# Nine weight blocks (three experts ahead) in one shared tensor, three slices of a modulation set computed in the routing gap, and expert borders with fewer register loads, in a two-layer inference step

## What is computed

```
for layer in (0, 1):
    shift, scale, gate = split(silu(c) @ w_ada[layer, 0] + b_ada[layer, 0], 3)   # c per sequence, w_ada is 1024 x 3072
    h = x * (1 + scale) + shift
    m = mixer(h)            # layer 0: gated linear attention beside a convolution; layer 1: pooling mixer
    x = layer_norm(ALPHA * x + (1 + gate) * m)
    shift, scale, gate = split(silu(c) @ w_ada[layer, 1] + b_ada[layer, 1], 3)
    h = x * (1 + scale) + shift
    comb = top-1 group of 4, then top-2 of its 4 experts, as weights      # 264 x 16
    m = sum over e of 16: ((silu(h @ w_gate[e]) * (h @ w_up[e])) * comb[:, e]) @ w_down[e]
    x = layer_norm(ALPHA * x + (1 + gate) * m)
```

## Time and profile before

| | us |
|---|---|
| median of 3 runs (lowest to highest) | 929.91 (926.99 to 933.59) |
| the profiled execution | 925.51 |
| its span in the profile | 923.7 |
| experts of layer 0 (24 chunks): first `gate_up` to the last `down`'s end | 246.30 to 509.41 |
| experts of layer 1 (25 chunks): the same | 637.42 to 891.46 |
| PE busy, share of the span | 86% |
| q1, the queue of SP's transfers | 271.74 MB, 74.7% of the span |

### The profile page before, as it was taken

One profiled execution on the slowest core, in us unless ns is written; L12 is line 12 of the kernel. 1 busy time (PEld: TensorE's weight loads), 2 busy tenths in 40 slices (PEclk: granted clock), 3 DMA queues, 4 the chain that ended last, 5 costly groups with the idle time before them and its releaser, 6 DMA issues.

```text
span 923.7 us, 22581 instructions
## 1 busy us (share of the span) xinstructions
PE 794.0 (86%) x9194; PEld 477.0 (52%) x9195; DVE 422.7 (46%) x1133; ACT 280.2 (30%) x562; POOL 129.6 (14%) x215
## 2 busy tenths in 40 slices
PE   4799999998699998797978879976999769999984
PEld 2478885784354444343433558743544434444443
DVE  1159988426344443333333461263444314444453
ACT  2045583314132322222221250141323112323323
POOL 0251777000011000000000000001010000101001
PEclk9799997999699999899988989997999979999997
DMA  9996633459307889999999999393699999998601
GB/s 321 381 261 234 223 141 106 172 191 390 149 0 285 345 360 421 420 425 419 427 416 411 360 388 370 144 382 137 274 377 418 428 418 426 420 420 364 272 0 47
DMA packets 63880, 280.39 MB, mean 304 GB/s; under 512 B 3013, under 2 KB 3627, under 8 KB 55638
## 3 DMA queue, kind: packets, MB, share of 16 engines
q1 hardware_dynamic: 60738, 271.74, 74.7%
q0 software_dynamic: 2432, 6.94, 2.5%
q10 hardware_dynamic: 676, 1.24, 0.4%
HBM read 277.47 MB, written 3.37 MB: 304 GB/s over the span
## 4 chain that ended last, share of the span: by engine, by line
PE 68%; DMA 20%; DVE 4%; issue 3%; ACT 3%; SPq 1%; POOL 0%; POOLq 0%; DVEq 0%; ACTq 0%
PE bank L605 18%; DMA ring<-in_w_up 15%; PE bank L715 8%; PE bank L615 7%; PE bank L854 6%; PE bank L577 6%; PE bank L627 6%; DMA ring<-in_w_ada 5%; PE bank L471 3%; PE bank L585 2%; PE bank L520 1%; PE bank L490 1%; PE bank L549 1%; PE bank L733 1%; DVE t L1191 1%
## 5 line engine op out<-in xcount | busy, mean ns | idle before, releaser
L605 PE MATMUL bank<-ring,work 128*32 128x256 f32 x3136 | 207.0, 408 | 60.7 <-DMA ring<-in_w_up 42.0
L605 PEld LDWEIGHTS bank<-ring,work 128*32 128x32 f32 x3136 | 106.0, 116 | 149.7 <-issue 105.4
L1609 DVE SCALAR_TENSOR_TENSOR x<-bank,ada,x 128x256 f32<-128x256 f32 x392 | 162.0, 476 | 0.0
L1606 DVE TENSOR_TENSOR work<-work,bank 128x32 f32<-128x32 f32 x98 | 18.4, 188 | 278.0 <-PE bank L627 278.0
L1765 POOL TENSOR_TENSOR work<-t 128x192 f32<-128x192 f32 x51 | 26.5, 519 | 618.4 <-PE bank L577 456.6
L615 PE MATMUL bank<-ring,work 128*32 128x256 f32 x1568 | 94.8, 382 | 0.0
L577 PE MATMUL bank<-htm,work 128*32 128x256 f32 (+1 forms) x1224 | 84.8, 391 | 9.6 <-POOL work L1768 9.6
L627 PE MATMUL bank<-work 32*128 32x264 f32 x816 | 77.6, 451 | 4.9 <-DVE x L1191 3.9
L1127 ACT ACTIVATE work<-bank 128x128 f32<-128x128 f32 x49 | 13.6, 278 | 217.4 <-PE bank L605 217.4
L715 PE MATMUL bank<-h,ring 128*128 128x264 f32 x320 | 73.9, 389 | 0.0
L715 PEld LDWEIGHTS bank<-h,ring 128*128 128x128 f32 x320 | 60.0, 190 | 11.5 <-issue 0.8
(11 more groups left out here) (242 smaller groups left out, 882.8 us busy)
## 6 DMA issues: line engine op xcount, KB each, us to landing
ring<-in_w_gate SPq DMA_DIRECT2D x32, 2048.0 KB, 13.0
ring<-in_w_up SPq DMA_DIRECT2D x32, 2048.0 KB, 16.4
ring<-in_w_down SPq DMA_DIRECT2D x32, 2048.0 KB, 17.5
ring<-in_w_ada SPq DMA_DIRECT2D x24, 2048.0 KB, 19.9
ring<-in_w_in_even SPq DMA_DIRECT2D x5, 2048.0 KB, 33.0
ring<-in_w_out_even SPq DMA_DIRECT2D x2, 2048.0 KB, 9.2
ring<-in_w_out_odd SPq DMA_DIRECT2D x2, 2048.0 KB, 20.8
htm<-in_x_prompt ACTq DMA_DIRECT2D x1, 1024.0 KB
```

Source lines behind the costliest of these rows:

```text
L605: last = mm(GU[C * q:C * (q + 1), :].rearrange("p (a n) -> p a n", a=2), hgc[:, P * (k % 2) + C * (k // 2):P * (k % 2) + C * (k // 2 + 1)] ...
L1609: last = v.scalar_tensor_tensor(out=x[:, i, 0:SEQ], in0=bank[4 + dq][:, 0:SEQ], scalar=gate[:, i, 0:1], in1=x[:, i, 0:SEQ], op0=ALU.mult, ...
```

## The change

- `big` is one SBUF tensor that holds `work`, `acc`, `t2` and `h`. Three further slots, 6 to 8, lie over its columns 3200 to 15488 (`late`): slots 6 and 7 over `work` and `acc`, slot 8 over `t2` and `h`. They are only used for experts. `prow` moves to `htm`, and POOL's fill of `htm` with zeros behind the first mixer's stores goes away.
- The order of the units and their slots is written out (`load_plan`, `PLAN`). Experts go through three sets of three slots (`SETS`), so expert e is issued once expert e-3 is done. Gate and up of an expert count on one semaphore.
- Before the experts of layer 0 SP issues, behind ada 11: ada 12, the gate of expert 1, ada 13, the up of expert 1, ada 14, gate and up of expert 0, the downs of experts 1 and 0, and expert 2. In layer 1 it is experts 0, 1 and 2, too.
- Units 12 to 14 are computed around `ranks(0)`; DVE takes them in with `ada_copy(2, 0)` behind the routing. Unit 15 alone is left behind the experts, and behind `layer_norm_var(1)`. PE waits for the copy before its first `turn`, since both use bank 3.
- Unit 7 is computed ahead of the output projection, unit 8 where unit 7 was, unit 10 ahead of the logits.
- In the first mixer the sums over the 256 prompt columns of the attention's output, and unit 4, come ahead of the products with the sample states; a table warm-up of ACT comes one step earlier; the final state has bank 0.
- In the expert loop on PE one number of the table is loaded per expert in place of two, and the counts to wait for are worked out once in three experts. Expert 15 stands behind the loop.

The diff, cut to its core:

```diff
@@ units, slots and the plan
-U_PRE = 19
+NSLOT = 9
 RING = 6
+LATE0 = 3200
+SETS = [[(4, 5, 0), (6, 7, 8), (1, 2, 3)], [(6, 7, 8), (0, 1, 2), (3, 4, 5)]]
+PIECES = [(0, 0, 4), (0, 4, 6), (1, 0, 4), (1, 4, 6), (2, 0, 3), (2, 3, 4), (2, 4, 6), (3, 0, 4), (3, 4, 6)]
+def load_plan():
+    plan = [(("ada", i), i) for i in range(4)]
...
+    plan += [(("ada", 12), 1), ((0, 1, 0), 6), (("ada", 13), 2), ((0, 1, 1), 7), (("ada", 14), 3), ((0, 0, 0), 4),
+             ((0, 0, 1), 5), ((0, 1, 2), 8), ((0, 0, 2), 0)]
+    plan += [((0, e, i), SETS[0][e % 3][i]) for e in range(2, EXPERTS) for i in range(3)]
+    plan += [(("ada", 15), 1), (("ada", 16), 2), (("ada", 17), 3), (("out1", 0), 4), (("out1", 1), 5), (("ada", 18), 0),
...
@@ SBUF
-        h = sb("h", [P, KD, T])
-        t2 = sb("t2", [P, KD, T])
-        acc = sb("acc", [P, KD, T])
-        work = sb("work", [P, 9152])
+        big = sb("big", [P, 9152 + 128 + 3 * KD * T])
+        work = big[:, 0:9152]
+        acc, t2, h = (big[:, a:a + KD * T].rearrange("p (k t) -> p k t", k=KD)
+                      for a in (9152, 9152 + KD * T + 128, 9152 + 2 * KD * T + 128))
+        late = big[:, LATE0:LATE0 + 3 * 4096].rearrange("p (s n) -> p s n", s=3)
@@ SP
             def fill_rest(l):
                 sp.wait_ge(M[l]["table_ready"], l + 1)
-                with sp.Fori(1, EXPERTS // 2) as ep:
-                    for j in range(2):
-                        e = sp.snap(2 * ep + j)
-                        chunks = sp.value_load(tab[l][0:1, bass.ds(e - 1, 1)], min_val=1, max_val=MAXCH)
+                with sp.Fori(1, EXPERTS // 3) as ep:
+                    for j in range(3):
+                        e = sp.snap(3 * ep + j)
+                        chunks = sp.value_load(tab[l][0:1, bass.ds(e - 2, 1)], min_val=1, max_val=MAXCH)
...
+            sp.wait_ge(E("mix0_stored"), 1)
+            sp.wait_ge(E("out0_src"), KD)
+            fill_expert(0, 1, 0)
+            unit_free(sp, ("ada", 13))
+            fill(("ada", 13))
+            sp.wait_ge(E("out0_done"), KD)
+            fill_expert(0, 1, 1)
+            unit_free(sp, ("ada", 14))
+            fill(("ada", 14))
+            for i in range(2):
+                unit_free(sp, (0, 0, i))
+                fill_expert(0, 0, i)
+            sp.wait_ge(E("tm_tr"), 2 * TT)
+            fill_expert(0, 1, 2)
+            unit_free(sp, (0, 0, 2))
+            fill_expert(0, 0, 2)
+            for i in range(3):
+                unit_free(sp, (0, 2, i))
+                fill_expert(0, 2, i)
@@ PE, expert loop
+                if l == 0:
+                    pe.wait_ge(E("ada_copied"), 5)
                 turn(1)
...
-                        lo = pe.value_load(tab[l][0:1, bass.ds(2 * ep + j, 1)], min_val=0, max_val=MAXCH)
-                        hi = pe.value_load(tab[l][0:1, bass.ds(2 * ep + j + 1, 1)], min_val=1, max_val=MAXCH)
-                        filled = [pe.snap((ep + ((u + i) // RING + 1)) * 16) for i in range(3)]
+                with pe.Fori(0, EXPERTS // 3) as ep:
+                    both_filled, filled = ([pe.snap(n * (ep + SET_FILLS[l][j])) for j in range(2)] for n in (32, 16))
+                    lo = bound(bass.ds(3 * ep, 1))
+                    for j in range(3):
+                        hi = bound(bass.ds(3 * ep + j + 1, 1))
+                        expert(j, lo, hi, both_filled[min(j, 1)], filled[min(j, 1)])
+                        lo = hi
@@ PE, around the routing of layer 0 and behind its experts
-            projection("out0", 0, U_OE, acc, 0, "out0_src", {})
             ada_unit(7)
+            projection("out0", 0, acc, 0, "out0_src", {})
+            ada_unit(8)
             layer_norm_var(0)
-            ada_unit(8)
             ada_unit(9)
             ada_columns()
+            ada_unit(10)
...
-            ada_unit(10)
             ada_unit(11)
+            pe.wait_ge(E("tm_a"), 4)
+            ada_unit(12)
+            ranks(0)
+            ada_unit(13)
+            ada_unit(14)
             ada_columns()
-            ranks(0)
             moe(0)
-            ada_unit(12)
             layer_norm_sum_x(1)
-            ada_unit(13)
             layer_norm_var(1)
-            ada_unit(14)
             ada_unit(15)
             ada_columns()
@@ DVE
             routing(0)
+            ada_copy(2, 0)
             moe(0)
```

281 lines of the change are left out of this document (149 added, 132 removed).

## The result

| | before | after |
|---|---|---|
| median (lowest to highest), us | 931.50 (926.99 to 933.59), 4 runs | 895.56 (893.59 to 897.72), 4 runs |
| ratio of the times | 1 | 0.9646, 95% interval 0.9605 to 0.9688 |
| the profiled execution | 925.51 | 897.72 |
| its span | 923.7 | 895.9 |

The changed kernel is 3.5% faster, 2.6 us from the forecast of 893. In a second set of runs it had 894.2 us beside 927.84 (13 runs of before), ratio 0.9642 (0.9587 to 0.9697).

The account below looks back on a forecast made before the run. The transfer queue was taken to bound the long middle of both expert stages, with PE following. Terms +1.1 - 15.0 - 5.4 - 15.0 - 1.8 = -36.1 us gave a forecast of 893 us, range 878 to 906.

Parts of the forecast that it names:

- Three experts ahead: Expert stages: expert 2 moves into the queue's idle window, one expert less in the queue-bound part; -15.0 us in each layer.
- Behind the experts: Layer 0, last `down` to first `h`: unit 15 starts earlier, 22.5 us in place of 27.9, so -5.4 us.
- The way to the first expert: Stretch up to layer 0's first `gate_up`: preloads and later projection cost +1.1 us in all, ends -2 and +10.
- Does it all fit ahead of the first chunk?: Preloads before layer 0's experts: start slips 0.3 us and first down 0.8, so +1.1 us.
- the next part: Front and routing gap: unit 7 +1.7, one unit fewer -2.5, units 13 and 14 +0.3; counted as 0, ends -3 and +3.
- PE's own gain on the way there: Before layer 0's experts: only unit 9 left behind the sum of squares, one unit goes, -2.5 us.
- The projection's slip: First mixer's output projection: unit 7 ahead of it, less some 0.7 us from earlier norm sums and warm-up, +1.7 us.
- Borders: Between experts on PE: one of two table loads goes; counts only behind layer 1's last wait, -1.8 us, ends 0 and -8.
- (a): Rival: preloads ahead of layer 0's experts collide, expert 0's down lands 10 us later; 903 us, chance 0.09.
- (b): Rival: the queue also loses its gaps in the expert stages, 8 us more in layer 0, 5 in layer 1; 880, chance 0.07.
- (c): Rival: late slots come free too late in layer 1, so its 15 us are lost; 908 us, chance 0.06.
- (d): Rival: PE must fetch code for the larger expert loop, at 3.5 us a border 18 us slower; 948 us, chance 0.04.

Follow-up runs that it names:

- x2: The changed kernel, but expert 2 is issued in the loop once expert 0 is done, so only two experts ahead: 924.9 us, ratio 0.9961.
- x4: The changed kernel with only half of the down matrix of layer 0's experts 3 to 15 transferred, the rest stale: 861.6 us in one run.
- x8: The changed kernel with six filling products, which nobody reads, around the last two scatters of each layer: 891.83 us, ratio 0.9613.
- x5: The changed kernel with SP's queue reordered: units 12 to 14, then expert 0 whole, then experts 1 and 2: 890.09 us, ratio 0.9592.
- x6: The changed kernel with unit 5 moved into PE's wait ahead of the column sums, units 6 and 7 one place forward: 890.89 us, ratio 0.9605.
- x9: The changed kernel with the edits of x5, x6 and x8 together: 881.36 us, ratio 0.9497.

## Why the prediction was right, and where it was not

**Three experts ahead: right.** -15.0 in layer 0 against -15.1, and in layer 1 -15.0 and -1.8 against -16.4. The reason given is the reason: x2 gives back the gain of the stages and leaves the rest, x4 shows that PE can do layer 0 in 222 us under the 247, and the last wait of layer 1 came 14.6 us earlier. The queue's idle time was forecast as 270 to 280; it was some 10 us, from 275.6 (expert 2's down, issued at 248.59, landed 27.0 us later) to expert 3's issue at 286.03.

**Behind the experts: right, with a wrong price inside.** The 27.9 us of the prediction's profile go from the last `down`'s start to `h`; in after it is 21.9 + 1.9 = 23.8, forecast 22.5. The missing 1.3 us is the clock: I took the norm's length from layer 1, where the sums L512 took 5.39 us, and in after they took 6.84. In neither place does a unit stand ahead of them, and without one they scatter between 5.25 and 6.84 us; with unit 12 among them before had 4.21 in layer 0. x8 shows that 3.8 is to be had. That the difference between the means is 5.4 all the same is because before waits longer there on average than in its first profile.

**The way to the first expert: the step that failed.** +1.1 was forecast and +6.6 came, by the means. Between the two profiles the first `gate_up` came at 252.3, where 246.6 was forecast: 5.7 us too late. Two things were wrong.

The larger is the output projection's slip, put at +1.7 and measured at 4.9 between the two profiles. It passes on in full: ada 11 is issued 31.0 us after the projection starts in before (200.46 and 169.46) and in after (205.32 and 174.34), and all seven blocks stand behind it. That is 3.2 of the 5.7 us.

The other is a consumer that was left out. "Does it all fit ahead of the first chunk?" compared only expert 0's blocks with the first `gate_up`, and the next part gave units 13 and 14 +0.3, as work inside a wait. It never asked when unit 14's weights land. By the prediction's own numbers that is 208.6 + 3 x 5.4 + 2 x 5.0 + 1.7 = 236.5. PE gets to unit 14 62.4 us after the projection starts (238.36 in after, where it ends with a slow unit 13, is 64.0; the second profile of after, x4 and x5 have 62.4), so with the projection where the prediction had it at 169.5 + 1.7 + 62.4 = 233.6. A wait of 2.9 us was due, and from the end of the wait to the first `gate_up` it is 11.3 us in after: 236.5 + 11.3 = 247.8 in place of 246.6, another 1.2 us. The rest, some 1.2 us, is that the blocks up to unit 14 took a little longer than reckoned. Its landing, from the issues at 221 and 230 (unit 14, and the up matrix of expert 0):

```profile
ring<-in_w_ada SPq DMA_DIRECT2D x1, 2048.0 KB, 19.7
...
ring<-in_w_up SPq DMA_DIRECT2D x1, 2048.0 KB, 20.4
```

Issued at 221.08, unit 14 landed 19.7 us later, at 240.8, and the gather behind it ran at 245.50. Expert 0's up matrix landed at 230.22 + 20.4 = 250.6 (forecast 246.6), 1.7 us before PE used it. So unit 14 was the last that the first chunk waited for, and the up matrix was close behind. x5 brings both forward and the whole 6.6 us are gone (244.4 against 245.3), though its projection is still 4.3 us later than the mean of before (168.6). PE's own gain on the way there, forecast as -2.5, is real, and larger: from the projection to the first `gate_up` it is 71.5 us in x5 and 76.8 in before. The two ends for this term were -2 and +10, and the +6.6 is inside.

**The projection's slip: mis-sized.** +1.7 was forecast, 4.9 came between the two profiles and 5.5 between the means. 3.3 of it is unit 7, which stands ahead of the projection now: it was reckoned as 2.4, but it waits 0.48 us for ACT and takes 2.37 us for 1.94. 0.9 is unit 6 (2.86 us for 1.93). The 0.7 that was to come back did come, as column sums that start 1.2 us earlier than in the first profile of before, but they take 1.8 us longer, so that 0.6 is lost in place of it. x6 wins back 3.6 by taking one unit out of this chain and putting it into the wait for DVE ahead of it.

**Borders: right inside the loop, too cheap at its end.** 0.2 and 0.7 us were forecast; measured are 0.05 inside the loop and 326.86 - 323.91 - 1.75 = 1.20 at its end. Each is some 0.1 to 0.75 us less than before's 0.8 and 1.3, so the loop's end was put 0.5 too low. Only the borders behind layer 1's last wait count, and they are 1.8 us shorter, the -1.8 of the sum; where the chunk behind that wait starts cold, 1.6 of it goes again.

**The rivals.** (a) is half true: the first chunk did slip, by 6.6 and not 10, yet by the late projection and unit 14's weights, and little by slower blocks or expert 0's down. The seven blocks took 37.3 us (213.3 to 250.6) where 36.3 were forecast. (b) is false, the slow slices are still there. (c) is false, layer 1 gained all of its 15 us. (d) is false: the border inside the loop is 1.80 us with three bodies, and the loop's end 2.95 for 3.02.

**By the medians.** 929.9 - 36.1 was within 2 us of 895.56, and that is partly luck: the term ahead of the experts was 5.5 us too good, and the profile behind the sum was 1.7 us of span under the mean of three, with the shortest norm and second mixer of them. The means of the spans differ by 31.4, the medians by 33.6 and 35.9 in the two sets. Where the remaining 2.2 to 4.5 us of the medians lie, no profile shows.

## What to carry to other kernels

Where a queue bounds a stage, look for the time in which it stands still before the stage, and count in blocks of queue: one expert moved into that window was worth one expert's transfer here, 15 us in each layer. Check every consumer of what is moved, not only the first and the last: a small step (unit 14) whose block stands behind others in an in-order queue can hold up the chain as well as the blocks of the stage itself. And where the queue's start hangs on a step of PE (the projection here), a unit put ahead of that step holds up PE's chain and the queue's together. And where PE idles ahead of a chain of sums on the critical path, a few products that nobody reads can be worth more than they cost, as in x8 and x9. The same stretch of before took 128.0, 130.7 and 133.3 us in three profiles, so profile before more than once.
